# Routing in two groups of tiles, the second layer's memory projection in the combination, and expert up weights in two transfers

## What is computed

```python
for l in range(DEPTH):
    h = x @ (w_in_a[l] if l < N_A_LAYERS else w_in_b[l - N_A_LAYERS])   # and w_kv_shared once
    tok = retention(...) or forgetting_attention(...)
    mem_out = memory_attention(mq, mem_k[l], mem_v[l])      # mem_k, mem_v = mem_prompt @ w_mem_kv[l]
    x = layer_norm(ALPHA * x + concat(tok, mem_out) @ w_o[l])
    x = layer_norm(ALPHA * x + hierarchical_moe(x, ...))

def hierarchical_moe(x, w_group, b_group, w_route, b_route, w_up, w_down):
    g_logits = t @ w_group + b_group;  g_idx = argmax(g_logits)
    g_w = softmax(g_logits)[g_idx]
    e_sel = (t @ w_route[g] + b_route)[g_idx]
    top_v, top_i = lax.top_k(e_sel, 2);  top_w = softmax(top_v) * g_w
    for e in range(32):                       # the two chosen ones of a token count
        gate, val = split(t @ w_up[e], 2)     # 1024 -> 2 x 256
        out += (silu(gate) * val * weight) @ w_down[e]   # 256 -> 1024
```

## Time and profile before

| | before |
|---|---|
| median of 3 runs | 1637.33 us |
| the profiled execution | 1630.63 us, span 1628.5 us |
| mean granted clock of PE | 0.868 of full speed |
| busy PE, DVE, ACT, POOL | 1295.0, 492.8, 359.3, 103.5 us |
| moved by DMA | 315.17 MB, mean 194 GB/s |

### The profile page before, as it was taken

One profiled execution on the slowest core, in us unless ns is written; L12 is line 12 of the kernel. 1 busy time (PEld: TensorE's weight loads), 2 busy tenths in 40 slices (PEclk: granted clock), 3 DMA queues, 4 the chain that ended last, 5 costly groups with the idle time before them and its releaser, 6 DMA issues.

```text
span 1628.5 us, 17691 instructions
## 1 busy us (share of the span) xinstructions
PE 1295.0 (80%) x7094; PEld 901.0 (55%) x7094; DVE 492.8 (30%) x1003; ACT 359.3 (22%) x727; POOL 103.5 (6%) x133
## 2 busy tenths in 40 slices
PE   6999998588849778873799989998588578888750
PEld 5999995456634223332799968784467433333220
DVE  2542136545330000006410137414533510000017
ACT  3012221441002111112212136412420111111110
POOL 0000001000001111102000020000000011111100
PEclk8999999788859989996897959899797779999885
DMA  7232213700269999965114040032600569999943
GB/s 277 79 116 78 91 40 100 236 1 26 96 284 400 424 425 422 421 269 197 39 41 160 27 156 1 19 118 61 196 14 26 240 252 427 424 424 423 422 178 111
DMA packets 93796, 315.17 MB, mean 194 GB/s; under 512 B 22290, under 2 KB 57250, under 8 KB 77090
## 3 DMA queue, kind: packets, MB, share of 16 engines
q1 hardware_dynamic: 80498, 283.90, 45.1%
q0 software_dynamic: 13232, 30.36, 5.0%
HBM read 299.58 MB, written 31.42 MB: 203 GB/s over the span
## 4 chain that ended last, share of the span: by engine, by line
PE 58%; DMA 24%; DVE 11%; ACT 4%; issue 1%; SPq 0%; POOLq 0%; DVEq 0%; ACTq 0%
DMA weight_ring<-in_w_up_dram 20%; PE ps L690 9%; PE ps L691 9%; PE ps L692 9%; PE ps L879 8%; PE ps L1155 2%; DMA work<-stream_rows,ints 2%; PE ps L1177 2%; PE ps L942 2%; PE ps L811 2%; PE ps L1223 1%; DVE small L1742 1%; PE ps L779 1%; PE ps L1167 1%; PE ps L895 1%
## 5 line engine op out<-in xcount | busy, mean ns | idle before, releaser
L879 PE MATMUL ps<-expert_weights,work 128*64 128x512 f32 x512 | 145.1, 731 | 54.6 <-DMA expert_weights<-in_w_up_dram 52.1
L1883 DVE TENSOR_TENSOR work<-ps,work 128x256 f32<-128x256 f32 x32 | 13.6, 425 | 472.7 <-ACT work L1412 472.7
L879 PEld LDWEIGHTS ps<-expert_weights,work 128*64 128x64 f32 x512 | 43.8, 167 | 154.6 <-issue 91.9
L879 PE MATMUL ps<-weight_ring,work 128*64 128x512 f32 x512 | 113.4, 594 | 14.4 <-DMA weight_ring<-in_w_up_dram 14.4
L691 PE MATMUL ps<-weight_ring_r,mix_cols_r 128*128 128x384 f32 (+3 forms) x360 | 121.0, 337 | 0.0
L692 PE MATMUL ps<-mix_cols_r,weight_ring_r 128*128 128x272 f32 x352 | 102.6, 292 | 0.0
L879 PEld LDWEIGHTS ps<-weight_ring,work 128*64 128x64 f32 x512 | 42.5, 137 | 84.8 <-issue 84.8
L1412 ACT ACTIVATE work<-ps 128x256 f32<-128x256 f32 x32 | 12.3, 383 | 282.0 <-PE ps L879 282.0
L690 PE MATMUL ps<-expert_weights_r 128*128 128x512 f32 (+1 forms) x160 | 68.9, 430 | 0.4 <-DVE mix_cols_r L1734 0.4
L691 PEld LDWEIGHTS ps<-weight_ring_r,mix_cols_r 128*128 128x128 f32 (+1 forms) x360 | 66.1, 184 | 4.2
L690 PE MATMUL ps<-weight_ring_r,mix_cols_r 128*128 128x384 f32 (+3 forms) x200 | 67.4, 338 | 0.7 <-ACT mem_kt L1459 0.7
(11 more groups left out here) (365 smaller groups left out, 2384.1 us busy)
## 6 DMA issues: line engine op xcount, KB each, us to landing
expert_weights<-in_w_up_dram SPq DMA_DIRECT2D x32, 2048.0 KB, 16.6
weight_ring<-in_w_up_dram SPq DMA_DIRECT2D x32, 2048.0 KB, 19.2
expert_weights<-in_w_down_dram SPq DMA_DIRECT2D x32, 1024.0 KB, 18.1
mix_cols<-in_w_down_dram SPq DMA_DIRECT2D x32, 1024.0 KB, 21.4
weight_ring<-in_w_in_a_dram SPq DMA_DIRECT2D x8, 1536.0 KB, 6.7
weight_ring<-in_w_o_dram SPq DMA_DIRECT2D x4, 2048.0 KB, 13.5
weight_ring<-in_w_kv_shared_dram SPq DMA_DIRECT2D x4, 1536.0 KB, 9.1
weight_ring<-in_cache_fox_k_dram SPq DMA_DIRECT2D x12, 384.0 KB, 5.0
```

Of the source, the lines that this page charges most:

```text
L879: last = mm(bank(0, rows=(t.start, t.stop)), xgT[:, k, t], WU[2 * q + j][:, k, :], start=(k == 0), stop=(k == KD - 1))
```

## The change

**Start.** The first memory chunk is now one of the two halves by rows: the weights come in two transfers of all 256 key columns and all 256 value columns of layer 0 only, and a block is one half of the memory times one of them (`mem_kv_block`, 8 matmuls). One block stands ahead of the transposes of x, one behind them, and two behind heads 2 and 5. The transposes of x use four banks at the start (`XB`), and x comes in two transfers, so that the first two tiles have a wait of their own.

**Memory of layer 1.** Its product leaves the projections. At the end of layer 0's experts, behind the last `down_done`, SP loads the memory rows again (two transfers of 0.5 MB) and the weights of layer 1 in one (2 MB); PE turns the rows and multiplies (`next_mem_kv`, 16 transposes and 16 matmuls of 512 columns) before the first tile of the combination.

**Routing.** Tiles 0 to 2 are one group, tiles 3 and 4 the other. The one-hots and ranks of the first are made while PE still works on the last tiles (`choose(0, 3)`, `to_slots(l, 0, 3)`). The slot of a token follows from its rank and the parity of its expert alone, so the first gather waits only for the token slots (16 columns of a matmul); weights and targets come next, and the chain over places and the lists for further blocks last, beside the first products.

**Experts.** Each up load is two transfers, for the first and last four of the eight K blocks, and PE waits for the first (`up_half`) before the product and for the second (`up_in`) in its middle. The last pair is unrolled out of the loop, and with it the seventeenth gather, its turn of rows and its copy are gone.

The core of the diff:

```diff
+XB = (4, 2, 4, 2)
 SP
-            def up_weights(l, e, b):
-                sp.dma_start(WU[b], w_up[l].rearrange("g e (p k) f -> p (g e) k f", p=P)[:, bass.ds(e, 1)]
-                             .rearrange("p a k f -> p (a k) f")).then_inc(S(f"up_in{b // 2}"), 16)
+            def up_weights(l, pair, q):
+                for half in range(2):
+                    k = slice(4 * half, 4 * half + 4)
+                    for b in (2 * q, 2 * q + 1):
+                        sp.dma_start(WU[b][:, k], w_up[l].rearrange("g e (p k) f -> p (g e) k f", p=P)
+                                     [:, bass.ds(pair * 2 + b % 2, 1), k].rearrange("p a k f -> p (a k) f")) \
+                            .then_inc(S((f"up_half{q}", f"up_in{q}")[half]), 16)
+            mem_weights(0)
+            sp.dma_start(X[:, 0:2, :], x_tiles[:, 0:2]).then_inc(S("x_in"), 16)
+            sp.dma_start(X[:, 2:ST, :], x_tiles[:, 2:ST]).then_inc(S("x_more"), 16)
...
             experts(0)
+            for m in range(2):
+                sp.dma_start(mem_rows1[m], mem_prompt[0, P * m:P * m + P]).then_inc(S("mem_in"), 16)
+            sp.dma_start(mem_w1, cols(w_mem_kv[1], 0, 2 * MW)).then_inc(S("mkv_w0"), 16)
             expert_rows(0, 0)
 POOL
-                    if i + 2 <= PAIRS:
+                    if i + 2 < PAIRS:
 PE
+            def pair(l, r, q, last_pair):
+                pe.wait_ge(S("xgt"), r * 2 + (s + q + 1))
+                pe.wait_ge(S(f"up_half{q}"), r * 32 + (16 * s + 32))
+                for k in range(KD):
+                    if k == KD // 2:
+                        pe.wait_ge(S(f"up_in{q}"), r * 32 + (16 * s + 32))
+                    for j in range(2):
...
+                    if i == NT - 1:
+                        pe.wait_ge(S("onehot"), 2 * l + 1)
+                        mm(ranks[:, 0:3], C("strict"), cnt[:, 0:3], start=True, stop=False)
...
+                slots_of(l, 0, 3)
+                mm(ranks[:, 3:5], C("ones"), earlier, start=True, stop=False)
+                pe.wait_ge(S("onehot"), 2 * l + 2)
...
+                slots_of(l, 3, NT).then_inc(S("slot_mm"), 1)
...
-                if h in (2, 5, 8):
-                    mem_kv_chunk((h + 1) // 3)
+                if h in (2, 5):
+                    mem_kv_block(2 + h // 5)
...
             experts(0)
+            next_mem_kv()
 DVE
+                    if i == NT - 1:
+                        to_slots(l, 0, 3)
                     if i:
                         route_tile(l, i - 1)
+                    if i == 3:
+                        link(choose(0, 3))
...
+                link(choose(3, NT))
+                to_slots(l, 3, NT)
+                weights_and_more(l)
```

More of the change, by code:

```diff
@@ L108, in shape_constants @@
     put("valid", valid)
+    e = np.arange(NE)
+    put("turn", np.tile(np.where(e % 2, 1, -1), (P, 1)))
+    put("first", np.tile(np.where(e % 2, SLOTS, SLOTS - 1), (P, 1)))
     r = i % 32
@@ L248, in cols @@
             return w[:, lo:hi].rearrange("(k p) n -> p k n", p=P)
[L250 to L253 removed]
+        mem_w0 = [view(big, 6 * TOK, KD, MW), view(big, 12 * TOK + KD * ML, KD, MW)]
+        mem_w1 = view(big, 6144, KD, 2 * MW)
+        memT1 = view(big, 10240, KD, ML)
+        mem_rows1 = [view(ring, KD * D, D), view(work, 3 * D, D)]
         chunks = []
@@ L280, in w_r @@
             if m == 10:
[L281 removed]
+                return view(big_r, 2048, KD, w)
             if (m % 2 == 0) == (m < CH_S):
@@ L316, in build @@
         gf = view(work, 320, NT)
[L317 to L323, removed]
+        ohg = view(work, 325, NT, NG)
+        ef = view(work, 345, 2, NT)
+        wj = view(work, 355, 2, NT)
+        first, s10, b10, p10 = [view(work, 365 + 10 * k, 10) for k in range(4)]
+        ex, gsum = view(work, 405, NT, NG + 1), view(work, 430, NT)
         oh = view(work, 450, 10, NE)
         oh_t = view(work, 770, 10, NE)
-        cnt = view(work, 1090, NT + 1, NE)
+        cnt = view(work, 1090, NT, NE)
         sums = [view(work, 1284 + 48 * k, 48) for k in range(2)]
@@ L329, in build @@
         place = view(work, 1412, NT, NE)
[L330 to L336, removed]
+        nxc = view(work, 1572, NE * 4)
+        lf = view(work, 1700, 17)
+        btx = view(work, 1720, 10, MORE)
+        earlier = view(work, 1880, 2, NE)
+        esw = view(work, 2048, NT * NG * EG)
+        ohs = view(work, 2208, 10, NE)
+        a1 = view(work, 2580, 10, P)
+        bt = view(work, 3860, 10, PAIRS)
+        bbt, bbw = view(work, 4020, 10, PAIRS), view(work, 7136, 10, 2 * PAIRS)
+        bbx = view(work, 4352, 10, 3 * MORE)
+        a1x = view(work, 5856, 10, P)
+        before = view(work, 7136, MORE, NE)
         gi = index_t[:, :]
@@ L827, in project_tile, with rank_bank, slots_of @@
                     last.then_inc(S("wo_mm"), 1)
+            def rank_bank(l):
+                return bank(6 - 2 * l, 0, NE * (NT + 1)).rearrange("p (i e) -> p i e", e=NE)
+            def slots_of(l, lo, hi):
+                for i in range(lo, hi):
+                    for n in (i, NT + i):
+                        last = mm(bank(7 - 2 * l, 0, PAIRS), a1[:, n, :], bbt[:, n, :], start=(n == 0),
+                                  stop=(n == 2 * NT - 1))
+                return last
             def project_and_route(l):
@@ L898, in experts @@
-                        last.then_inc(S("down_done"), 1)
+                        pair(l, r, q, False)
+                for q in range(2):
+                    pair(l, PAIRS // 2 - 1, q, q == 1)
                 more = pe.value_load(lists[0:1, 16:17], min_val=0, max_val=MORE)
-                pe.wait_ge(S("xgt"), g + PAIRS + 1)
+                pe.wait_ge(S("xgt"), s + PAIRS)
                 pe.wait_ge(S("y_ev"), s + PAIRS + 1)
+                pe.wait_ge(S("places"), 4 * l + 4)
+                for n in range(10):
+                    last = mm(bank(7, 0, 3 * MORE), a1x[:, n, :], bbx[:, n, :], start=(n == 0), stop=(n == 9))
@@ L902, in experts @@
+                last.then_inc(S("slot_mm"), 1)
+                pe.wait_ge(S("slots"), 3 * l + 3)
                 pe.sem_inc(S(f"more_step{l}"), 1)
```

361 lines of the change are left out of this document (208 added, 153 removed).

## The result

The changed kernel takes 1599.22 us (median of four runs, 1595.49 to 1601.51) against 1636.82 us for the kernel before (four runs): a ratio of 0.976, 95% interval 0.9733 to 0.9788. The forecast was 1606, range 1588 to 1621. The profiled execution took 1598.18 us with a span of 1596.3, 32.2 us less than the span before; the sum had -30.9. The total is right, but four terms (routing, stream, tail and combination) are each off by 2.5 to 4.7 us, and 3.6 us came where the sum had none; that these errors nearly cancel is luck. The views of the changed kernel follow in the order of the earlier trace rows.

A forecast was written before the change was run, and what follows sets the result against it. No engine bounds the whole: PE bounds the projections, a DVE chain the routing, DMA bytes the experts. Terms -6.5, -13.8, -15.0, -7.1, +8 and +3.5 sum to -30.9, giving 1599.7, plus 6.7 to the median: 1606 us, range 1588 to 1621.

The forecast's parts named there:

- routing: From last router tile to first up product: earlier slots and gather start the byte-bound rest 7.5 us earlier per layer, -15.0.
- stream: Expert up loads after the restart: halved loads mean shorter rows and more packets, +4 us per layer, +8.
- tail: End of each layer's experts: only half a product follows the last up transfer, -3.55 us per layer, -7.1.
- combination: After layer 0's last down product: memory loads share DMA with scatter and expert rows, +3.5 us, bounds +1 and +15.
- Start: Before the first product: four banks and half a memory chunk ahead of the transposes start it 6.5 us earlier.
- projections: Layer 1's memory product leaves them: three 6.91 us stretches become two of 3.46, -13.8 us.
- Rival E: Projections: weight preparation becomes the bound and the 13.8 us return as PE waits for DVE; 1620 us, chance 0.05.
- Rival A: First gather of the experts waits out the weight stream, so routing gives nothing; 1621 us, chance 0.09.
- Packets: Expert weight stream: 19 ns fixed per packet, 224 more packets per engine and layer, taken as +4 us per layer.
- B: Experts and combination: both prices at their upper end, packets 6.2 us per layer and combination +15; 1622 us, chance 0.09.
- C: All runs smoothly: gathers as alone (-10), packets free (-8), first product faster (-2); 1586 us, chance 0.08.
- D: Expert stream: each added transfer stalls it by its own fixed time, 157 us in all; 1763 us, chance 0.03.

The follow-up runs named there:

- e5: Changed kernel, but each layer's first gather also waits for the second group of slot results (weights and targets), issued 6.4 us later: 1609.46 us.
- e1: Changed kernel, but each up load is one whole transfer again, with one wait on PE before the product: 1605.26 us.
- e3: Changed kernel, but each up load is four transfers with 4 KB rows, PE still waiting twice: 1604.69 us.
- e4: Changed kernel, but layer 1's memory loads are issued once layer 0's last up load has landed, ahead of the last down product: 1593.15 us.

## Why the prediction was right, and where it was wrong

**Start, right; projections, right in kind.** The start came within the bounds (5.0 to 7.6 for 6.5). The memory product left the projections as forecast, and the 2.4 us of the slow first product, which the prediction saw and counted as nothing, came too: 2.2 at the higher clock. Rival E is out, with PE idle for 1.9 of 178.3 us.

**The 3.6 us lost before the router need not be the change's.** The same code took from 223.1 us (e5) to 228.7 (e1) from the first retention matmul to the last router tile, 226.9 in the changed kernel and 226.2 on average in nine executions. The one profile of the kernel before has 223.4, inside that span but near its low end, so a part that belongs to the change can't be ruled out. One place is found, worth 1.8 us. In the chain of the changed kernel four matmuls of the last sample head take twice what they took before:

```profile
260.98 3.72 PE ps L1110 x4
```

```profile
284.46 1.92 PE ps L1052 x4
```

The granted clock was 0.50 there (1.2 GHz) and 1.00 before (2.4 GHz). In the changed kernel PE had waited 2.33 us for the state of this head, and in e1, where it waited 1.98, the four take 3.77 us; in e5 it waited 0.69, and they take 1.98. So these matmuls differ between executions of the same code; where the rest of the 3.6 us went stays open.

**Routing, right, with a part that belongs to the halves.** The forecast was 7.5 per layer with a gather of 10.5. With whole loads (e1) it is 8.0 and 7.4 us with a gather of 11.1 and 10.5, so this term was right with the loads that it was worked out for. The further 1.9 and 2.4 come from the shorter packets beside the gather: 11.1, 8.6 and 7.7 us with rows of 16, 8 and 4 KB. The prediction had this only as a bound of -1 on the packets' price. Its "a gather alone takes 5.49 us" was misread: by the earlier trace rows the DMA share was 0.98 until 474.4, 4.1 us after that gather's issue, so it flew beside the last rows of the backlog (of 4 KB), and no run shows a first gather alone. In the packet records the gather's own rows start to move 4.4 us after its issue in e1, the changed kernel and e3 alike, and then take 6.0, 3.4 and 2.5 us from first to last; only this part follows the rows beside it. The Trainium skill (DMA: Bandwidth & Descriptors, "Queues, rings and completion order") says that a DMA engine takes turns between its queues a whole packet at a time. If so, a gather waits out longer turns where the rows beside it are longer (each row is one packet record in the trace), and the three runs agree: the flights differ by 2.1 to 2.5 us between rows of 16 and 8 KB and by 0.9 to 1.0 between 8 and 4 KB, and each is six to eight times what one row takes longer (303 and 151 ns, from the records in e3's section). Rival A is out: in the changed kernel the gather lands at 445.8 while the backlog runs on to about 455 (a share of 0.61 of the 10 us from 449).

**Packets: the failed term.** "Which leaves 19 ns fixed per packet" was read from stretches of 4 to 10 us with other things in them, and is 9 ns in streams of 230 us. The price is 2.0 per layer, not 4.

**Tail, right against the right kernel.** Half a product went, but in layer 0 the last down weights land 0.5 us after PE could use them, and the product took 5.36 us instead of 3.67, so only 1.3 is left there against the kernel before; in layer 1 it is 3.3. Against whole loads in the new kernel it is 3.0 and 5.0, on average 4.0 for a forecast of 3.55. Halves as a whole were forecast at +0.45 per layer and gain 4.1.

**Combination: the mis-sized term.** "At 394 GB/s 3.1 MB end at about 744, the rows' 1 MB behind them at about 748.5": the scatter, which must land before the rows leave, lost 5.9 us to 3.1 MB issued 2 us ahead of it, where the sum let it run beside them; and PE's product, "just enough" by the forecast, ended too late. It came to +7.4, inside the bound of +15; e4 shows that 5.5 of it are where the loads stand. The scatter lost more than turns beside rows of 4 and 2 KB would cost by the measure of the first gather (eight turns of 162 ns, 1.3 us, an estimate): its own rows start to move 5.1 us after its issue instead of 1.6 and then take 3.1 instead of 1.3. Why it starts so late no run shows.

**The other rivals.** B had the combination larger, as it came, but its packets at 6.2. C's undisturbed gather and free packets did not come. D had each added transfer stall the stream; 56 of them per layer cost 4.2 us in e3, packets included, less than 0.1 us each where D decides from 0.55 on.

## What to carry to other kernels

A small gather beside a bulk stream in another queue was priced here by the size of the stream's rows: shorten the rows where the small one flies and at the last product, and leave them long between. That does not price every small transfer: the last scatter of layer 0 went from 3.2 to 9.1 us beside rows of 4 and 2 KB. What is moved into an idle stretch must have landed before the short chain in it starts. And an operation's time read from a stretch of a few us (19 ns per packet) needs a longer stretch, or a run that doubles it, before it carries a term.

## What the runs showed of the hardware that was not expected

- The first gather, of the same rows, takes 11.1, 8.6 or 7.7 us beside rows of 16, 8 or 4 KB.
- An added packet in a queue that is never empty costs 9 ns per engine in the stream, and 56 added transfers per layer, by the 9 ns record that each leaves on an engine, 0.5 us of the 4.2.
- The last scatter of layer 0 takes 9.14 us beside 3.1 MB of loads in rows of 4 and 2 KB, and 3.20 without them; most of the difference passes before its first row moves.
- The same 16 matmuls at the very start take 3.72 us in one execution and 5.6 to 6.2 in another, with a granted clock of 1.00 in the trace both times (changed kernel and e4); the cause is open.
